# Weights that land in place in a two-loop attention layer, a bias that goes through DRAM, and two orders on TensorE

## The chip, the cores and the metric

One core of a Trainium2 chip runs the whole program. The metric is the device time of one execution in microseconds (us), lower is better. The kernel before takes 3244.75 us, the median of three runs (3242.59 to 3246.57).

## The reference, cut to what matters

One inference step of two layers, for a prompt of 2048 rows and a sample of 32 rows, in float32, model width 1024.

Layer 0 (here "layer AB"): an RMS norm, one input projection `h @ w_in`, then two head groups on the result.

- Group A is a gated linear attention: 4 heads, keys of 64, values of 128, a low-rank decay gate (`glow @ w_gate_up + b_gate`, log-sigmoid, divided by 16), a state that is carried from rows to rows, a per-head RMS norm and a SiLU gate z_a.
- Group B is a sliding-window attention: 8 query heads of 64, 2 key heads, window 128, scores plus a relative-position bias (a table of 32 buckets by 8 heads), a softmax with a learned sink, a SiLU gate z_b.
- The outputs of both are concatenated, multiplied by `w_out` and added to x.

```
h = rms_norm(x, rms_g)
q_a, k_a, v_a, glow, z_a, q_b, k_b, v_b, z_b = _split(h @ w_in, SPLIT_AB)
s = einsum(q, k) * HD_B ** -0.5 + bias ;  p = sink_softmax(s, sink)
return x + concat([o_a * silu(z_a), o_b * silu(z_b)]) @ w_out, ...
```

Layer 1 (a Mamba-2 block) follows. It takes the larger part of the time, and no instruction of it is changed.

## The kernel before, in words

The rows are worked on in 17 tiles: tile 0 is the sample (32 rows), tiles 1 to 16 are 128 rows of the prompt each. The program runs in blocks one after another, each with its own semaphores, with a barrier of all engines between two (`give_back`): `setup`, `layer_gla` (group A, here "the first loop"), `layer_swa` (group B and the output projection, "the second loop"), `layer_c`, `project_c`. Data goes from block to block through DRAM.

Each engine's order is written out by hand as `start(x, n)`, 16 times `step(x, n, m)` and `end(x)`; x is the tile that is finished, n the next, m the one after that. SP issues all transfers of the loops, in this order too, and a wait in SP's list holds up all that stands behind it. Engines wait on counters: `since(pe, s["za_made"], x, 1)` waits until the tile before x has been through that stage.

A float32 product of full accuracy is made from three products of rounded operands: high by high, high by low, low by high. So each weight matrix is split once: ScalarE (ACT) writes the high half (`weights_high`, a Copy that rounds, for `w_in` with the norm's scale), and VectorE (DVE) writes the low half, raw minus high (`weights_low`). The raw rows come in through a staging buffer, one k of 8 (128 of the 1024 rows) at a time:

- First loop: 1808 columns, `stage_a` with three places. ACT issues the first three k in `setup`; SP issues the other five in `layer_gla`, each once the low half of the k three before is made (L342). In `project`, TensorE (PE) waits in the sample's first product for the low half of each k.
- Second loop: 1024 columns of `w_in`, then `w_out`, through two places that are a view of `sc`, the tile of the attention scores (`stage`, L853). So the first scores of the loop wait for all 16 low halves. SP's list has the load of tile 1 (`load_h(n)`) behind all of them.

`setup` also makes the bias: PE and DVE build `frep`, a row of offsets per head; SP writes it to DRAM (`skew`), waits, and reads it back shifted by one element per partition into `bias`; DVE adds the band mask, and the block ends.

Orders on PE that the change touches:

- First loop, `step`: `queries_keys(n)`, `attention(x)`, `values(n)` (gate columns into bank VG, then the values into bank V0), `gate_low(n)`, `outputs(x)`, `turn_qk(n)`, `gate_up(n)`, `turn_x(m)`, `gate(n)` (z_a, in the same bank as the queries and keys), `turn_oa(x)`. `queries_keys(n)` waits for `za_made` of the tile before, DVE's last read of that bank.
- Second loop, `step`, where `before` is the tile before x: `scores(x)`, `queries(n)`, `turn_weights(x, 0)`, `turn_x1(before)`, `gate(n)`, `steps_in(before)` (L1472, reads h1T, which DVE writes), `turn_weights(x, 1)`, `weighted(x, 0)`, `time_step(before)`, `output_start(x, 0)`, `weighted(x, 1)`, `output_start(x, 1)`, `turn_ob(x)`, `turn_q(n)`, `turn_k(n)`, `output_end(x)`. ACT's list after `steps_in` is: `time_step(before)`, `window_gate(n)` with two table loads, then `weights_turned(x, 1)`, the copy that `weighted(x, 1)` reads. DVE's is: `weights_turned(x, 1)`, `weighted(x, 0)`, `time_step_tok(before)`, `window_gate(n)`, `weighted(x, 1)`.

## Time and profile before

| what | value |
|---|---|
| median of three runs | 3244.75 us |
| the profiled execution | 3245.2 us, its span 3243.4 us |
| TensorE: matmul busy, weight load busy | 2931.4 us (90%), 2485.5 us (77%) |
| DVE, ACT, POOL busy | 1876.6 (58%), 1412.8 (44%), 61.3 us (2%) |
| mean granted TensorE clock | 0.968 |
| DMA | 87 GB/s over the span |

The span runs from the first instruction to the last. A line of a timeline gives start and duration in us, the engine, the source line, the operation, what it writes and reads, and in brackets how long its engine was idle before it and what ended that. SPq is SP's own list. A matmul's duration is longer than its distance to the next one, because matmuls overlap; the pace is read from the starts. "issue" as a releaser means that the profile shows nothing the engine waited for. The blocks begin at these times: the first loop at 34.13 us, its 16 steps at about 88 us, the second loop at 557.84 us, layer 1 at 1355.76 us.

### The profile page before, as it was taken

Reading aid. Unit: us, or ns where it says so; the run is one execution under the profiler, and the core shown is the slowest. Engines: PE = TensorE matmul, PEld = TensorE weight load, DVE = VectorE, ACT = ScalarE, POOL = GpSimd, SP = SyncE. Lnnn points to the kernel's source line nnn. Section 1 sums busy time; section 2 is a strip of 40 time slices with the busy share of each in tenths; the row PEclk is TensorE's granted clock in tenths of the full one; section 3 lists DMA queues with packets and bytes.
Section 4 is the critical chain, followed back from the end, with each engine's and each line's share of the span. In section 5 each row is a group of like instructions: output and inputs, shape, how many; then the busy total and the mean of one; then the engine's idle time right before and its main releaser. Section 6 shows DMA issues by size and latency. Waiting matters only on the chain. (4 is left out here: it accounts for less than half of the span.)

```text
span 3243.4 us, 50025 instructions
## 1 busy us (share of the span) xinstructions
PE 2931.4 (90%) x18074; PEld 2485.5 (77%) x18074; DVE 1876.6 (58%) x4799; ACT 1412.8 (44%) x2901; POOL 61.3 (2%) x166
## 2 busy tenths in 40 slices
PE   4999996688888888599999999999999999879999
PEld 2788886266666666489997999889997999758787
DVE  3343343344443444268887888878887888842322
ACT  2455553333333333245555555545555555521211
POOL 0000000000000000000000000000000000000000
PEclk9999998699999999799999999999999999989999
DMA  4122212322212221332213221142123211144443
GB/s 144 71 83 82 82 71 71 122 73 82 82 65 75 79 80 59 127 114 65 64 60 102 83 64 59 51 133 65 59 62 100 66 61 60 53 170 137 131 145 111
DMA packets 148699, 280.87 MB, mean 87 GB/s; under 512 B 46359, under 2 KB 69402, under 8 KB 144378
## 3 DMA queue, kind: packets, MB, share of 16 engines
q1 hardware_dynamic: 147042, 276.55, 26.0%
q10 hardware_dynamic: 1560, 3.05, 0.3%
q8 instruction: 58, 0.95, 0.1%
q14 instruction: 39, 0.32, 0.0%
HBM read 204.29 MB, written 75.26 MB: 86 GB/s over the span
## 5 line engine op out<-in xcount | busy, mean ns | idle before, releaser
L2060 PEld LDWEIGHTS bank<-hT_c,w_group 128*128 128x128 f32 x6528 | 749.5, 192 | 39.1 <-issue 33.5
L2060 PE MATMUL bank<-hT_c,w_group 128*128 128x128 f32 x6528 | 750.9, 275 | 0.0
L1884 DVE SCALAR_TENSOR_TENSOR conv_acc<-u,convw,conv_acc 128x128 f32<-128x128 f32 (+1 forms) x1224 | 331.4, 339 | 10.4 <-ACT conv_acc L1818 8.0
L2047 PE MATMUL bank<-wz_high,h_high 128*128 128x512 f32 (+1 forms) x544 | 239.2, 440 | 13.5 <-DVE wz_low L1965 13.5
L708 PE MATMUL bank<-wa_high,hT_high 128*128 128x512 f32 (+5 forms) x544 | 191.0, 351 | 43.2 <-DVE za L622 26.0
L2285 PE MATMUL bank<-wout_high,yT_high 128*128 128x512 f32 (+1 forms) x544 | 212.6, 391 | 6.4 <-DVE wout_low L2254 6.4
L2047 PE MATMUL bank<-wz_low,h_high 128*128 128x512 f32 (+1 forms) x544 | 215.3, 396 | 0.0
L2047 PE MATMUL bank<-wz_high,h_low 128*128 128x512 f32 (+1 forms) x544 | 214.9, 395 | 0.0
L2285 PE MATMUL bank<-wout_low,yT_high 128*128 128x512 f32 (+1 forms) x544 | 212.5, 391 | 0.0
L2285 PE MATMUL bank<-wout_high,yT_low 128*128 128x512 f32 (+1 forms) x544 | 212.5, 391 | 0.0
L708 PE MATMUL bank<-wa_low,hT_high 128*128 128x512 f32 (+5 forms) x544 | 187.2, 344 | 0.0
L708 PE MATMUL bank<-wa_high,hT_low 128*128 128x512 f32 (+5 forms) x544 | 187.1, 344 | 0.0
L2218 ACT ACTIVATE yT_high<-yT_in 128x2048 fp32r<-128x2048 f32 (+1 forms) x34 | 62.6, 1841 | 275.1 <-PE bank L2285 260.8
L1772 ACT ACTIVATE u<-bank 128x256 f32<-128x256 f32 (+1 forms) x68 | 25.5, 376 | 323.0 <-PE bank L2060 323.0
L1818 ACT ACTIVATE conv_acc<-u,vec,convw 128x128 f32<-128x128 f32 (+1 forms) x408 | 162.4, 476 | 7.0 <-ACT u L1772 3.0
L2262 DVE TENSOR_TENSOR x_in<-x_in,bank 128x512 f32<-128x512 f32 (+1 forms) x34 | 23.4, 687 | 220.6 <-PE bank L2285 220.6
L708 PEld LDWEIGHTS bank<-wa_high,hT_high 128*128 128x128 f32 (+1 forms) x544 | 100.3, 184 | 64.5 <-issue 34.1
L1434 PE MATMUL bank<-wout_high_ab,oT_high 128*128 128x512 f32 (+1 forms) x272 | 110.6, 407 | 38.6 <-DVE oT_low L1221 20.6
L1385 PE MATMUL bank<-wb_high,h0T_high 128*128 128x512 f32 (+1 forms) x272 | 117.2, 431 | 29.7 <-DMA h0T_low<-h0T_low_d 20.4
L2047 PEld LDWEIGHTS bank<-wz_high,h_high 128*128 128x128 f32 (+1 forms) x544 | 101.7, 187 | 51.8 <-issue 30.6
L2103 PE MATMUL bank<-xdt,ed 128*128 128x128 f32 (+1 forms) x1088 | 132.7, 275 | 3.1 <-DVE ed L1941 3.1
L2103 PEld LDWEIGHTS bank<-xdt,ed 128*128 128x128 f32 (+1 forms) x1088 | 125.9, 187 | 5.6 <-DVE ed L1941 5.3
(289 smaller groups left out, 5812.1 us busy)
## 6 DMA issues: line engine op xcount, KB each, us to landing
hT_c<-h1T SPq DMA_DIRECT2D x64, 512.0 KB, 3.3
acb<-acT SPq DMA_DIRECT2D x64, 512.0 KB, 3.7
yT_in<-yT SPq DMA_DIRECT2D x32, 1024.0 KB, 5.2
yT<-yT_t SPq DMA_DIRECT2D x64, 256.0 KB, 3.1
xin<-in_x_prompt SPq DMA_DIRECT2D x16, 512.0 KB, 3.7
h0T_high_d<-hT_high SPq DMA_DIRECT2D x16, 512.0 KB, 2.6
h0T_low_d<-hT_low SPq DMA_DIRECT2D x16, 512.0 KB, 3.4
h0T_high<-h0T_high_d SPq DMA_DIRECT2D x16, 512.0 KB, 3.4
```

The costliest lines, as they stand in the source:

```text
L708: ins = M(out, h[x.buf][:, k, 0:x.R], wt[:, k, col:col + n], start=(k == 0 and p == 0), stop=(k == KT - 1 and p == 2))
L1385: ins = M(out, h[:, k, 0:x.R], wt[:, k, col:col + 512], start=(k == 0 and p == 0), stop=(k == KT - 1 and p == 2))
L1434: ins = M(B_OUT[n][0:x.R, :], y[:, k, 0:x.R], wt[:, k, 512 * n:512 * n + 512], start=(k == 0 and p == 0), stop=(k == KT - 1 and p == 2))
L1772: A(ub[:, 4:6, 3:3 + R], B_BC[:, 0:2 * P].rearrange("p (j r) -> p j r", j=2)[:, :, 0:R], ACT.Copy).then_inc(s["u1_made"], 1)
L1818: ins = A(acc[:, i, 0:R], ub[:, i, 3:3 + R], ACT.Identity, scale=c["convw"][:, 3 * CT + ct:3 * CT + ct + 1], bias=c["vec"][:, V_CB + ct:V_ ...
L1884: ins = V.scalar_tensor_tensor(acc[:, i, 0:R], ub[:, i, tap:tap + R], c["convw"][:, tap * CT + ct:tap * CT + ct + 1], acc[:, i, 0:R], ALU. ...
L2047: ins = M(B_Z[0:x.R, :], h[:, k, 0:x.R], wt[:, k, :], start=(k == 0 and p == 0), stop=(k == KT - 1 and p == 2))
L2060: ins = M(out, wg[x.g % 2][:, k, j * P:(j + 1) * P], hT[x.buf][:, k, :], start=(k == 0), stop=(k == KT - 1))
L2103: ins = M(B_INTRA[h // 4][0:R, (h % 4) * P:(h % 4 + 1) * P], ed[0:R, h, 0:R], xdt[0:R, (h // 2) * P:(h // 2 + 1) * P], start=True, stop=True)
L2218: nc.scalar.activation(yh[x.buf][:, :, 0:x.R], yT[x.buf][:, :, 0:x.R], ACT.Copy).then_inc(s["y_high"], 1)
L2262: V.tensor_tensor(x[0:R, :], x[0:R, :], psum[cur.buf][0:R, :], ALU.add).then_inc(s["sum_made"], 1)
L2285: ins = nc.tensor.matmul(psum[i][0:R, :], y[:, k, 0:R], wt[:, k, :], start=(k == 0 and p == 0), stop=(k == K - 1 and p == 2))
```

## The change

- The raw weights of the first loop get a tensor for all 8 k (`raw_a`), which lies at the address of the low half (`two_views`: one tensor is given back, and the other allotted in its place). DVE then writes the low half over the raw rows. SP and ACT issue all 8 k in `setup`, SP the even and ACT the odd ones. The sample's rows are loaded there too.
- The same for the second loop: `raw_b` is allotted for both loops. SP loads all 8 k of `w_in`'s other columns in `start` of the first loop, behind `store_h(n)` and ahead of step 0. Once the low half of a k is made, `w_out` of that k is loaded into the same place, where its low half will lie. `sc` is no staging buffer any more.
- `frep` is a view of `raw_b`. ACT writes it to DRAM at the end of `setup` and nothing there waits for it. `bias` and `band` are read in `start` of the second loop, and POOL adds them.
- First loop on PE: the gate columns are a stage of their own, `values_gate`, ahead of `queries_keys`; it needs no `za_made`.
- Second loop on PE: `steps_in(before)` goes behind `weighted(x, 0)`, `time_step(before)` behind `weighted(x, 1)`; the wait for `dtok_made` goes from `output_start(x, 0)` to `output_start(x, 1)`.

```diff
+def two_views(nc, stack, raw, low, shape):
+    with ExitStack() as first:
+        r = first.enter_context(nc.sbuf_tensor(raw, shape, F32))
+    return r, stack.enter_context(nc.sbuf_tensor(low, shape, F32R))
...
+            w["raw_b"], w["wout_low"] = two_views(nc, ab, "wb_raw", "wout_low_ab", [P, KT, DM])
...
+                w["raw_a"], w["wa_low"] = two_views(nc, gla, "wa_raw", "wa_low", [P, KT, A_W])
...
@@ setup @@
+        def weights(eng, k):
+            raw = w["raw_a"][:, k, :]
+            eng.dma_start(raw[:, 0:QB], wv[k][:, 0:QB]).then_inc(c["wa_in"][k], 16)
+            eng.dma_start(raw[:, QB:A_W], wv[k][:, KB:ZB]).then_inc(c["wa_in"][k], 16)
...
-            sp.wait_ge(s["offsets_copied"], HB)
-            sp.dma_start(d["skew"], frep[:, :, :]).then_inc(s["skew_out"], 16)
-            sp.wait_ge(s["skew_out"], 16)
...
-            sp.dma_start(w["bias"][:, :, :], skewed).then_inc(s["bias_in"], 16)
+            sp.dma_start(w["xin"][0:DEC, :], a["x_sample"][0]).then_inc(c["x_in"], 16)
+            for k in range(0, KT, 2):
+                weights(sp, k)
...
-            dve.wait_ge(s["bias_in"], 16)
-            nc.vector.tensor_tensor(w["bias"][:, :, :], w["bias"][:, :, :],
-                                    band[:, :].unsqueeze(1).to_broadcast([P, HB, 2 * P]), ALU.add).then_inc(s["set_dve"], 1)
...
+            for k in range(1, KT, 2):
+                weights(act, k)
             act.wait_ge(s["params_in"], 16 * n_in)
             nc.scalar.activation(c["acol"][:, :], alog[:, :], ACT.Exp).then_inc(s["exp_a"], 1)
+            act.wait_ge(s["offsets_copied"], HB)
+            act.dma_start(d["skew"], frep).then_inc(c["skew_out"], 16)
@@ layer_gla, SP @@
+            def next_weights():
+                sp.wait_ge(c["skew_out"], 16)
+                for k in range(KT):
+                    raw = w["raw_b"][:, k, :]
+                    sp.dma_start(raw[:, 0:512], wv[k][:, QB:KB]).then_inc(c["wb_in"][k], 16)
+                    sp.dma_start(raw[:, 512:DM], wv[k][:, ZB:D_AB]).then_inc(c["wb_in"][k], 16)
...
             def start(x, n):
-                load_x(x)
...
                 load_x(n)
-                for k in range(3, KT):
-                    weights(k)
                 store_h(x)
                 store_kv(x)
                 store_h(n)
+                next_weights()
@@ layer_gla, PE @@
             def start(x, n):
...
+                values_gate(x)
                 queries_keys(x)
                 values(x)
...
             def step(x, n, m):
+                values_gate(n)
                 queries_keys(n)
                 attention(x)
                 values(n)
@@ layer_swa, SP @@
             def weights(k):
-                if k >= 2:
-                    sp.wait_ge(s["w_low"], k - 1)
...
+                sp.wait_ge(s["w_low"], k + 1)
+                sp.dma_start(raw[:, k, :], wo[k]).then_inc(wo_in[k], 16)
...
             def start(x, n):
                 load_h(x)
-                weights(0)
-                weights(1)
                 load_kv(x)
...
-                for k in range(2, KT):
-                    weights(k)
+                sp.dma_start(bias[:, :, :], skewed).then_inc(s["bias_in"], 16)
+                sp.dma_start(band[:, :], a["c_band"]).then_inc(s["bias_in"], 16)
                 load_oa(x)
                 residual(x)
-                for k in range(KT, 2 * KT):
+                for k in range(KT):
                     weights(k)
@@ layer_swa, POOL @@
+            pool.wait_ge(s["bias_in"], 32)
+            nc.gpsimd.tensor_tensor(bias[:, :, :], bias[:, :, :],
+                                    band[:, :].unsqueeze(1).to_broadcast([P, HB, 2 * P]), ALU.add).then_inc(s["bias_made"], 1)
+            pool.wait_ge(s["bias_made"], 1)
+            nc.gpsimd.tensor_copy(bprev[:, :, :], bias[:, :, 0:P]).then_inc(s["init0"], 1)
@@ layer_swa, DVE scores @@
                 if x.sample:
-                    dve.wait_ge(s["w_low"], 2 * KT)
+                    dve.wait_ge(s["bias_made"], 1)
@@ layer_swa, PE @@
             def output_start(x, n):
                 if n == 0:
                     pe.wait_ge(s["oa_in"], 32 * x.t + 32)
+                    since(pe, s["h2_half"], x, 1, 2)
+                else:
                     since(pe, s["dtok_made"], x, 1)
-                    since(pe, s["h2_half"], x, 1, 2)
                 partial(x, n, 0)
...
                 gate(n)
-                if before is not None:
-                    steps_in(before)
                 turn_weights(x, 1)
                 weighted(x, 0)
                 if before is not None:
-                    time_step(before)
+                    steps_in(before)
                 output_start(x, 0)
                 weighted(x, 1)
+                if before is not None:
+                    time_step(before)
                 output_start(x, 1)
```

## Rows read from the trace of the kernel before

**Rows 1.** Windows, second loop's steps: length, busy per engine, clock, DMA share, GB/s
```profile
640.00:1340.00 700.00, 592.71 (x3028) 465.20 (x3026) 290.68 (x684) 233.24 (x606) 31.49 (x49) 0.97 0.21 73
```

**Rows 2.** Waits of PE, 0 to 600 us: sum, times, longest
```profile
PE bank L708 <- DVE za L622: 26.0, 16, 1.7
```

**Rows 3.** Waits of PE, 640 to 1340 us
```profile
PE bank L1472 <- DVE h1T_t L1250: 50.0, 16, 3.4
...
PE bank L1434 <- issue: 18.0, 16, 1.2
```

**Rows 4.** Timeline, end of setup and start of the first loop
```profile
21.09 0.13 DVE L229 TENSOR_SCALAR acol<-acol 32x1 f32<-32x1 f32 x1
...
31.06 2.29 DVE L232 TENSOR_TENSOR bias<-bias,band 128x2048 f32<-128x2048 f32 x1 [9.84 <-DMA bias<-skew]
...
36.49 1.06 ACT L421 ACTIVATE xn<-xin 32x1024 f32<-32x1024 f32 x1 [1.07 <-DMA xin<-in_x_sample]
```

**Rows 5.** Timeline, the first loop's weights
```profile
43.29 6.13 DVE L565 SCALAR_TENSOR_TENSOR wa_low<-stage_a,vec,wa_high 128x1808 fp32r<-128x1808 f32 x3 [1.40 <-ACT wa_high L414]
...
66.61 2.10 DVE L565 SCALAR_TENSOR_TENSOR wa_low<-stage_a,vec,wa_high 128x1808 fp32r<-128x1808 f32 x1 [1.99 <-ACT wa_high L414]
...
69.20 0.63 PE L708 MATMUL bank<-wa_low,hT_high 128*32 128x512 f32 x1
...
73.46 0.42 PE L708 MATMUL bank<-wa_high,hT_high 128*32 128x272 f32 x1
...
74.71 0.28 PE L744 MATMUL bank<-wa_high,hT_high 128*32 128x256 f32 x1
```

**Rows 6.** Timeline, a step of the first loop
```profile
311.34 1.28 DVE L579 TENSOR_TENSOR hT_low<-bank,hT_high 128x512 fp32r<-128x512 f32 x2
...
315.29 0.47 PE L708 MATMUL bank<-wa_high,hT_high 128*128 128x512 f32 x1 [1.64 <-DVE za L622]
```

**Rows 7.** Timeline, tile 2's rows in step 0
```profile
90.73 1.06 ACT L421 ACTIVATE xn<-xin 128x1024 f32<-128x1024 f32 x1 [0.40 <-DMA xin<-in_x_prompt]
```

**Rows 8.** Windows, five us of bulk loads at the start of layer 1
```profile
1365.00:1370.00 5.00, 1.08 (x3) 0.52 (x4) 1.92 (x4) 2.58 (x5) 0.00 (x0) 0.50 1.05 394
```

**Rows 9.** Timeline, start of the second loop
```profile
557.84 1.28 ACT L1102 ACT_TABLE_LOAD   x1 [5.67 <-PEq L65]
...
565.19 1.28 DVE L1163 SCALAR_TENSOR_TENSOR wb_low<-sc,vec,wb_high 128x1024 fp32r<-128x1024 f32 x1 [12.23 <-ACT wb_high L1013]
...
567.32 0.69 PE L1499 MATMUL bank<-ident,kdup 128*128 128x128 f32 x2 [15.87 <-DMA wdt<-in_w_in_c]
...
596.03 0.43 PE L1486 MATMUL bank<-ident,qn 32*128 32x32 f32 x4
...
599.79 2.36 DVE L1166 TENSOR_TENSOR wout_low_ab<-sc,wout_high_ab 128x1024 fp32r<-128x1024 f32 x2 [2.10 <-ACT wout_high_ab L1015]
...
620.90 1.67 DVE L1179 TENSOR_TENSOR sc<-bank,bias 32x320 f32<-32x320 f32 x4
...
623.04 0.79 PE L1385 MATMUL bank<-wb_high,h0T_high 128*128 128x512 f32 x1 [20.44 <-DMA h0T_low<-h0T_low_d]
...
630.39 0.55 PE L1415 MATMUL bank<-ident,sc 32*128 32x32 f32 x8
```

**Rows 10.** Timeline, a step of the second loop
```profile
932.36 1.94 PE L1472 MATMUL bank<-h1T_t,wdt 128*32 128x128 f32 x16 [3.02 <-DVE h1T_t L1250]
...
934.23 1.09 PE L1415 MATMUL bank<-ident,sc 128*128 128x128 f32 x8
...
938.47 0.47 PE L1434 MATMUL bank<-wout_high_ab,oT_high 128*128 128x512 f32 x1 [1.12 <-issue]
...
938.60 0.60 ACT L1039 ACTIVATE pT<-bank 128x512 f32<-128x512 f32 x1
...
941.32 0.38 PE L1425 MATMUL bank<-vprev,pT 128*128 128x128 f32 x2
...
943.02 0.48 PE L1434 MATMUL bank<-wout_high_ab,oT_high 128*128 128x512 f32 x1
```

More of the change, by code:

```diff
@@ L137, in program @@
         c["wc_in"] = nc.alloc_semaphore("wc_in")
-        c["wa_in"] = [nc.alloc_semaphore(f"wa_in{i}") for i in range(3)]
+        c["wa_in"] = [nc.alloc_semaphore(f"wa_in{i}") for i in range(KT)]
+        c["wb_in"] = [nc.alloc_semaphore(f"wb_in{i}") for i in range(KT)]
+        c["x_in"], c["skew_out"] = nc.alloc_semaphore("x_in"), nc.alloc_semaphore("skew_out")
         with ExitStack() as ab:
             w = {}
-            w["bias"] = sb("bias", [P, HB, 2 * P], ab)
-            w["wdt"] = sb("wdt", [P, KT, HC], ab)
+            w["raw_b"], w["wout_low"] = two_views(nc, ab, "wb_raw", "wout_low_ab", [P, KT, DM])
             with ExitStack() as gla:
                 w["wup"] = sb("wup", [RANK, HA * DK], gla)
-                w["stage_a"] = sb("stage_a", [P, 3, A_W], gla)
+                w["xin"] = sb("xin", [P, DM], gla)
+                w["raw_a"], w["wa_low"] = two_views(nc, gla, "wa_raw", "wa_low", [P, KT, A_W])
                 give_back(nc, setup(nc, a, c, d, w, psum))
@@ L340, in _ @@
             wv = a["w_in_ab"][0].rearrange("(k p) n -> k p n", p=P)
-            def weights(k):
-                sp.wait_ge(s["w_low"], k - 2)
-                sp.dma_start(stage[:, k % 3, 0:QB], wv[k][:, 0:QB]).then_inc(w_in[k % 3], 16)
-                sp.dma_start(stage[:, k % 3, QB:A_W], wv[k][:, KB:ZB]).then_inc(w_in[k % 3], 16)
+            def next_weights():
[4 more added lines that the diff above has]
+                    sp.dma_start(raw[:, 512:DM], wv[k][:, ZB:D_AB]).then_inc(c["wb_in"][k], 16)
             def load_x(x):
-                if not x.fixed or x.t > 0:
-                    sp.wait_ge(s["xn_made"], x.t)
-                sp.dma_start(xin[0:x.R, :], a["x_sample"][0] if x.sample else xp[x.t - 1]).then_inc(s["x_in"], 16)
+                sp.wait_ge(s["xn_made"], x.t)
+                sp.dma_start(xin[0:x.R, :], xp[x.t - 1]).then_inc(c["x_in"], 16)
             def store_h(x):
@@ L738, in attention, with values_gate @@
                 ins.then_inc(s["kd_full"], 1)
+            def values_gate(x):
+                pe.wait_ge(s["h_low"], 2 * x.t + 2)
+                project(B_VG[0:x.R, 0:A_VG], x, A_V1, A_VG, s["vg_full"])
             def values(x):
-                project(B_VG[0:x.R, 0:A_VG], x, A_V1, A_VG, s["vg_full"])
                 for k in range(KT):
@@ L832, in sb @@
             return ctx.enter_context(nc.sbuf_tensor(name, shape, dtype))
-        bias, wdt = w["bias"], w["wdt"]
-        bprev = sb("bprev", [P, HB, P])
+        bias, bprev, band = sb("bias", [P, HB, 2 * P]), sb("bprev", [P, HB, P]), sb("band", [P, 2 * P])
+        wdt = sb("wdt", [P, KT, HC])
         wh, wl = sb("wb_high", [P, KT, DM], F32R), sb("wb_low", [P, KT, DM], F32R)
-        vh, vl = sb("wout_high_ab", [P, KT, DM], F32R), sb("wout_low_ab", [P, KT, DM], F32R)
+        vh, vl = sb("wout_high_ab", [P, KT, DM], F32R), w["wout_low"]
+        raw = w["raw_b"]
         hh, hl = sb("h0T_high", [P, KT, P], F32R), sb("h0T_low", [P, KT, P], F32R)
@@ L1010, in weights_high @@
             def weights_high(k):
-                act.wait_ge(w_in[k % 2], 32 * (k // 2 + 1))
                 if k < KT:
-                    A(wh[:, k, :], stage[:, k % 2, :], ACT.Copy, scale=c["vec"][:, V_RMS0 + k:V_RMS0 + k + 1]).then_inc(s["w_high"], 1)
-                else:
-                    A(vh[:, k - KT, :], stage[:, k % 2, :], ACT.Copy).then_inc(s["w_high"], 1)
+                    act.wait_ge(c["wb_in"][k], 32)
+                    A(wh[:, k, :], raw[:, k, :], ACT.Copy, scale=c["vec"][:, V_RMS0 + k:V_RMS0 + k + 1]).then_inc(s["w_high"], 1)
+                else:
+                    act.wait_ge(wo_in[k - KT], 16)
+                    A(vh[:, k - KT, :], raw[:, k - KT, :], ACT.Copy).then_inc(s["w_high"], 1)
             def softmax(x, half):
```

53 lines of the change are left out of this document (18 added, 35 removed).

## The prediction

> **What bounds the kernel now.** I read the windows by stage first, then PE's waits, then the timeline of single steps. Layer AB ends at 1352 us of 3243, and nothing after it is changed, so only what moves its end counts. In the second loop's steps [rows 1] PE's matmuls are busy 592.7 of 700 us, DVE 290.7, ACT 233.2, DMA a fifth: PE sets the pace there and the others count only where PE waits for them. PE's waits in the steps are few and regular: 26.0 us in 16 waits for `za` in the first loop [rows 2]; 50.0 us in 16 for h1T and 18.0 us in 16 for "issue" in the second [rows 3]. The last are at `output_start(x, 0)`, where PE really waits for `dtok_made`: the matmul starts at 938.47 [rows 10], 0.11 us after DVE's copy ends. The two starts are different: there PE idles for tens of us behind weights that come in through few staging places. So three things can be won: setup and the first start, the second start, and the steps' waits.
>
> **Setup and start of the first loop.** The last work of the block now is the bias, which ends at 31.06 + 2.29 = 33.35; without it DVE's small instructions end at 21.22 [rows 4]: 12.1 us earlier. The readback, 9.84 us of that, goes to the second loop. x of the sample is loaded in setup, so ACT's wait of 1.07 goes [rows 4]. What is late next is ACT's norm of that tile, unchanged. Then the weights: from DVE's first low half at 43.29 to its last at 66.61 + 2.10 = 68.71 pass 25.4 us. DVE's pace without waits is 6.13 / 3 = 2.04 [rows 5], so eight take 16.3, if all eight are there: 7.4 MB from 5.5 us on at about 390 GB/s [rows 8] are in after 19 us, at 24.5, and DVE's first low half is due at 43.29 - 12.1 - 1.1 = 30.1. That makes 9.1 more, and the last low half at 46.4. On the other side stands the order on PE. Before, the 24 matmuls of 512 columns ran between the low halves and only one group of three was left; now the 24 of 272 columns do, and the 24 of 512 come behind the last low half. PE paces them at 0.43 us (half clock, 69.20 against its neighbours) until it has worked without a gap from 68.7 to 73.5; after that 0.23 [rows 5]. So: 0.7 for the last group, to 47.1; 9.5 matmuls at 0.43 until 51.2; 14.5 at 0.23, to 54.6. The values start there, against 74.71 [rows 5]: 20.1 us won. Bounds: 22.3 if PE is quick at once, 15 if ACT, which now issues half the weights and the skew, is held up by a full queue.
>
> **Steps of the first loop.** `values_gate(n)` needs `h_low` alone, which DVE has made at 311.34 + 1.28 = 312.6, while PE comes free at 315.29 - 1.64 = 313.65 [rows 6]. It runs 24 x 0.125 = 3.0 us, and `za` is made at 315.1, inside that. So all 26.0 us [rows 2] go. What is late next: `gate_low(n)` waits for ACT's copy of the gate columns, which comes behind ACT's norm of tile m (its x lands late in each step) and two copies; by the timeline ACT is through about 2.5 us before PE asks. Bounds 16 (if that margin is wrong by one us in each step) and 28. I take 26.0.
>
> **The preload of 4 MB.** Its 16 issues on SP stand ahead of `load_x` of tile 2. They need 4.2 MB / 390 GB/s = 10.7 us [rows 8], then that tile 1.4, and x lands some 8.2 us later relative to its step than at 90.7 [rows 7]. ACT is in order: norm (3.7 us), then copies of queries, keys, gate. PE does not ask for the gate's copy before it is through 24 + 24 + 48 matmuls, so of 8.2 us I find 0.5 left on the path. Every further us of landing time costs one. Loss 0.5, bounds 0 and 7 (at 275 GB/s, as just after the start of the second loop, it is 15 us). The preload is over by step 1.
>
> **Start of the second loop.** Weights are there. ACT begins after its table load, at 557.84 + 1.28 = 559.1; low halves at DVE's pace of 1.28 [rows 9] are ready from 561.6 to 570.7. PE needs the small loads before: the last of these (`wdt`) is the eleventh issue of the block and released PE at 567.32 [rows 9]; with four weight issues (2.2 us) less ahead, 565.1. Queries and gate of the sample are 48 matmuls: 11 at 0.43, 37 at 0.23, 13.2 us, so PE's `turn_q` at 578.7 against 596.03 [rows 9]: 17.3 won. ACT then starts the high halves of `w_out` at 581.4 (2.7 later, as before), and all of `w_out` has landed: its loads are issued from 565 to 571 and need 11 us. DVE started its first at 599.79 and its second ended 2.36 later, 1.18 each [rows 9]: first at 582.5, eight end at 591.9, and scores start there instead of 620.90: 29.0 won. SP is free to send `load_h(1)` right after `vcur` is copied (581.0 instead of 617.2), so `queries(1)`, 7.3 us long (623.04 to 630.3), ends at 594.7. Then PE waits for the exponentials: scores to exponentials took 5.5 us on DVE and ACT, so `turn_weights(0)` is at 597.4 instead of 630.39 [rows 9]: 33.0 won. The bias lands near 569, and POOL's add, which DVE did in 2.29 [rows 4], is wanted at 591.9: hidden by 15 us or more. Bounds 26 (loads of small rows as slow as before, `w_out` at 275 GB/s) and 36.
>
> The Trainium skill speaks against this add: "SBUF — State Buffer", section "Who interferes with whom", says that a DVE instruction with two SBUF inputs and a GpSimd one that reads SBUF lock each other out for a whole instruction, and "GPSIMD Engine Reference", section "Performance versus the Vector engine", gives 4.5 us for the add. By these the seventh or eighth low half would end some 4 us later and PE's queries 2.2 us, and the forecast would be 3149; no row of before shows two such instructions at once.
>
> **Steps of the second loop.** Now PE waits 3.02 us for h1T, until 932.36 [rows 10]. `turn_weights(x, 1)` (0.92) and `weighted(x, 0)` (1.8) move in there; ACT and DVE have made what they need at 929.6. So `steps_in` starts at 932.4 as before and ends at 934.23. `output_start(x, 0)`, 12 matmuls or 2.85 us (938.47 to 941.32), ends at 937.1. But `weighted(x, 1)` needs ACT's copy that starts at 938.60 and takes 0.60 [rows 10], and this hangs on `steps_in` through ACT's time step and two table loads, which do not move. PE waits 2.1 us there, starts at 939.25, and with 1.70 (941.32 to 943.02) is through at 940.95. `time_step(before)` and DVE's copy of `dtok` make 0.8 more, and `output_start(x, 1)` starts at 941.8 against 943.02 [rows 10]: 1.24 us per step, 15 steps with a tile before: 18.6. In `end` the order stays and only the wait for `dtok` (1.1) is covered: 1.1. Sum 19.7. Bounds: 0, and 4.1 x 15 = 62, if neither wait came back.
>
> **Sum.** 20.1 + 26.0 - 0.5 + 33.0 + 19.7 = 98.3. From the profiled execution's 3245.2, 0.45 above the median, that is 3146.9: 3147.
>
> **Rivals.** *The transfers bound it* (12%): they gain at most where queues have room. For it: SP's issues of large loads at the start of layer 1 stood for up to 6 us each. ACT's skew then leaves only when the weights are in (24.5 instead of 20.4, 4 us), the preload runs at 275 GB/s (5 us), and `w_out` and the small loads give back 7: 3163. Against it: loads of 128 long rows were issued at 0.45 to 0.85 us. *Nothing comes out of the second loop's order* (14%): PE's waits only move to `weighted(x, 1)` and `dtok`, as DVE and ACT, in order, shift with PE: 3147 + 18.6 = 3166. *Both waits go* (8%), if ACT's copy is earlier than I read: 43 us better, 3104. *It does not do what it says* (2%): if the raw tensors are not free when their loads are issued, setup waits anyway; then the starts' 53 us are gone, 3200. *Slower* (2%): the new wait of 2.1 us ahead of `weighted(x, 1)`, inside a stretch that had short waits only, drops PE's clock to half. A step has 13.6 us of matmuls from there to the next scores' end; at half clock 15 steps cost 204 us and the time is 3351. It decides from 6.5 us of work at half clock per step on (98.3 / 15). Against it: the wait of 3.02 us at about the same place leaves the clock at 0.97 [rows 1].
>
> **How the numbers follow.** The forecast, 3147 with its own range of 3128 to 3162, has 62%. A measurement here tells 0.2% (6.5 us) from no change. All cases but the last are faster by more than that: faster 97%; slower 2%; 1% for a mixture that ends within. The range of 8 in 10 takes in the second rival and the first: 3125 to 3178.
>
> **What would show it.** Right: `norm` of the sample at 23.4 us; last low half of the first loop near 46.4; no wait for `za`; second loop's block about 45 us earlier and its first scores at DVE 34 us after the block's start (63 before); PE's wait for h1T under 0.4 us, and a new one of about 2 us for ACT's `pT`. Wrong: ACT's x wait in step 0 over 12 us; a step of the second loop of 41.8 us as before; a clock under 0.9 in a loop.

## The result, and the profile after

The changed kernel takes 3149.84 us (median of 4, 3145.83 to 3151.18) against 3243.67 for the kernel before (median of 4, 3238.45 to 3246.57): a ratio of 0.971, 95% interval 0.9694 to 0.9727. The forecast was 3147. Its profiled execution took 3149.56 us with a span of 3147.8, against 3245.2 of before: 95.6 us less.

The sum comes out within 3 us, but two of its terms are wrong in opposite directions. All times in this table are read from the two profiled executions, as the distance between the same event before and after. `oa_high` is ACT's copy of a tile's finished outputs of group A, one per tile, so the distance of two is one step of the first loop:

```
                               predicted   measured
setup and first start            20.1        19.5
first loop's steps               26.0        30.2   (16 x 1.89)
preload of 4 MB in step 0        -0.5       -10.3
second start                     33.0        33.2
second loop's steps              19.7        27.2
layer 1 (unchanged)               0          -4.2
sum                              98.3        95.6
```

The preload's term is what closes the balance at the first `oa_high`, 11.2 us earlier than before (107.44 against 118.65). The start gave 19.5 and step 0 its share of the steps' term, about 2.0, so 19.5 + 2.0 - 11.2 = 10.3 were lost on the way. Experiment 1 measures it directly. From its first matmul to the end, layer 1 took 1884.4 us before and 1888.6 after; over the profiled executions of all twelve kernels, which have the same code there, it is 1881.7 to 1888.7. So the last term is scatter of that size.

**First start.** The timeline after, end of setup and the first loop's weights (start, length, engine, line, operation; in brackets the wait ahead of it), answers [rows 4, 5]:

```profile
23.50 1.05 ACT L423 ACTIVATE xn<-xin 32x1024 f32<-32x1024 f32 x1
...
30.30 16.19 DVE L567 SCALAR_TENSOR_TENSOR wa_low<-wa_raw,vec,wa_high 128x1808 fp32r<-128x1808 f32 x8 [1.40 <-ACT wa_high L416]
...
47.23 0.63 PE L710 MATMUL bank<-wa_high,hT_high 128*32 128x512 f32 x1
...
52.35 0.50 PE L710 MATMUL bank<-wa_high,hT_high 128*32 128x512 f32 x1
...
55.22 0.28 PE L748 MATMUL bank<-wa_high,hT_high 128*32 128x256 f32 x1
```

The norm starts at 23.50 (23.4 was forecast), all eight low halves are one row without a gap, 16.19 long, and end at 46.49 (46.4). The 24 matmuls of 512 columns start at 47.23, the pace turns from 0.43 to 0.23 at 52.35, and the values start at 55.22 instead of 74.71.

**First loop's step.** From one tile's `oa_high` to the next it is 26.19 us now (317.12 to 343.31, for one). This window is as long as one step: length, busy time of PE, PE's weight loads, DVE, ACT, POOL, clock, DMA share, GB/s.

```profile
311.34:337.53 26.19, 26.19 (x173) 23.57 (x172) 10.91 (x34) 14.57 (x38) 0.00 (x0) 1.00 0.23 85
```

PE is busy in all of it. The wait for `za`, 26.0 us in 16 before [rows 2], is gone, and the step takes 26.19 instead of 28.08.

**Step 0, where the preload lies.** SP's queue and then ACT and PE:

```profile
66.41 0.79 SPq L350 DMA_DIRECT2D wb_raw<-in_w_in_ab  x1
67.24 1.19 SPq L351 DMA_DIRECT2D wb_raw<-in_w_in_ab  x1
...
75.11 0.45 SPq L351 DMA_DIRECT2D wb_raw<-in_w_in_ab  x1
75.60 0.44 SPq L355 DMA_DIRECT2D xin<-in_x_prompt  x1
```

The waits of PE in the first loop after (engine, line, what it waited for: sum, times, longest), and windows behind the first of them:

```profile
PE bank L755 <- ACT v_tok L448: 4.6, 1, 4.6
```
```profile
88.40:93.00 4.60, 4.55 (x17) 1.52 (x17) 0.00 (x0) 0.73 (x2) 0.00 (x0) 0.50 0.08 29
93.00:98.00 5.00, 5.00 (x17) 3.35 (x16) 1.54 (x5) 1.87 (x10) 0.00 (x0) 0.50 0.00 0
98.00:103.00 5.00, 5.00 (x21) 4.28 (x20) 4.31 (x14) 4.83 (x15) 0.00 (x0) 0.76 0.00 0
103.00:108.00 5.00, 5.00 (x32) 4.23 (x31) 3.21 (x9) 2.96 (x4) 0.00 (x0) 1.00 0.54 211
```

The 16 issues hold SP from 66.41 to 75.56, so x of tile 2 is issued at 75.60; ACT, in order, stands for it 12.9 us, until 83.7. ACT's copy of the gate columns (L448) comes behind it, and PE waits 4.6 us for that copy. Then it runs at half clock (0.50, the lower of its two levels) for 9.6 us, and for part of the next five, in which the mean is 0.76. The granted clock, the last figure but two of a row, is the one to read: PE is "busy" in all of it.

**Second start.** Timeline after, answering [rows 9]:

```profile
518.44 1.28 ACT L1106 ACT_TABLE_LOAD   x1 [5.41 <-PEq L65]
...
525.13 0.69 PE L1504 MATMUL bank<-ident,kdup 128*128 128x128 f32 x2 [12.83 <-DMA wdt<-in_w_in_c]
...
529.59 5.46 POOL L981 TENSOR_TENSOR bias<-bias,band 128x2048 f32<-128x2048 f32 x1 [10.05 <-DMA band<-in_c_band]
...
539.04 0.44 PE L1491 MATMUL bank<-ident,qn 32*128 32x32 f32 x4
...
542.80 9.58 DVE L1170 TENSOR_TENSOR wout_low_ab<-wb_raw,wout_high_ab 128x1024 fp32r<-128x1024 f32 x8 [2.10 <-ACT wout_high_ab L1019]
...
546.63 0.50 PE L1389 MATMUL bank<-wb_high,h0T_high 128*128 128x512 f32 x1 [2.55 <-DMA h0T_low<-h0T_low_d]
```

From the block's start at 518.44 it is 6.7 us to PE's release by `wdt` (7.3 forecast), 20.6 to `turn_q` (20.9), 24.4 to the first low half of `w_out` (24.7), and `turn_weights(0)`, at 557.79, is 39.4 us after the start (39.6 forecast; 72.6 before). Only `queries(1)` came by another way: PE waited 2.55 us for its rows and ran at half clock for 3.3, but the exponentials were later still.

**Second loop's step.** Timeline of one step after, answering [rows 10], and PE's waits from 560 to 1270 us, answering [rows 3]:

```profile
852.60 1.93 PE L1477 MATMUL bank<-h1T_t,wdt 128*32 128x128 f32 x16 [0.47 <-DVE h1T_t L1254]
...
858.83 0.60 ACT L1043 ACTIVATE pT<-bank 128x512 f32<-128x512 f32 x1
...
859.48 0.49 PE L1429 MATMUL bank<-vprev,pT 128*128 128x128 f32 x2 [2.01 <-ACT pT L1043]
...
862.09 0.50 PE L1438 MATMUL bank<-wout_high_ab,oT_high 128*128 128x512 f32 x1 [0.32 <-DVE dtok_t L1273]
```
```profile
PE bank L1429 <- ACT pT L1043: 29.8, 15, 2.0
...
PE bank L1477 <- DVE h1T_t L1254: 11.2, 16, 3.0
...
PE bank L1438 <- DVE dtok_t L1273: 4.7, 15, 0.3
```

The wait for h1T shrank from 3.02 to 0.47 (under 0.4 forecast), and the new one for ACT's `pT` is 2.01 (2.1 forecast). The steps take 40.8 to 41.05 us, but for one of 43.76. Before, they were of two kinds: 41.8 to 42.2 and, in about two of three, 43.3 to 43.8. One of the long kind in windows, then the five us in which h1T is waited for and the five behind them, all of the kernel before:

```profile
946.47:990.21 43.74, 37.38 (x190) 29.52 (x189) 18.27 (x43) 14.78 (x39) 1.95 (x3) 0.96 0.22 76
970.00:975.00 5.00, 1.70 (x11) 1.12 (x10) 4.25 (x13) 0.95 (x3) 0.00 (x0) 0.99 0.54 177
975.00:980.00 5.00, 5.00 (x31) 4.26 (x30) 1.23 (x4) 2.12 (x4) 0.00 (x0) 0.67 0.34 138
```

Behind the wait the clock is 0.67 in the mean, that is, at half for some 3.3 of the five us. The steps without a drop went from about 42.0 to 40.9 us, so the change took 1.1 us of waits out of each, and nearly everywhere this drop too, 1.7 us in each long step. The forecast had only the first.

The one long step of the changed kernel shows that the new wait can bring a drop as well. It is this wait for `pT` with the matmuls behind it, and the whole step:

```profile
652.08 0.49 PE L1429 MATMUL bank<-vprev,pT 128*128 128x128 f32 x2 [1.99 <-ACT pT L1043]
```
```profile
655.00:660.00 5.00, 4.68 (x12) 3.62 (x12) 1.15 (x3) 0.00 (x0) 0.21 (x1) 0.50 0.03 7
627.83:671.59 43.76, 39.07 (x191) 30.79 (x189) 18.17 (x44) 14.78 (x38) 1.96 (x3) 0.92 0.22 72
```

### The profile page after: what moved, and what is told of

It is laid out like the page before. It is cut to its first block and busy times, and to the rows that moved or that the text cites. A ratio compares the mean times of both kernels' runs of the same rounds, so it can differ in the third digit from the quotient of the medians.

```text
span 3147.8 us, 50003 instructions
## 1 busy us (share of the span) xinstructions
PE 2924.8 (93%) x18074; PEld 2485.2 (79%) x18074; DVE 1870.8 (59%) x4798; ACT 1411.4 (45%) x2901; POOL 67.9 (2%) x167
## 5 line engine op out<-in xcount | busy, mean ns | idle before, releaser
L2052 PE MATMUL bank<-wz_high,h_high 128*128 128x512 f32 (+1 forms) x544 | 240.0, 441 | 12.9 <-DVE wz_low L1970 12.9
L2267 DVE TENSOR_TENSOR x_in<-x_in,bank 128x512 f32<-128x512 f32 (+1 forms) x34 | 23.4, 687 | 219.8 <-PE bank L2290 219.8
L1438 PE MATMUL bank<-wout_high_ab,oT_high 128*128 128x512 f32 (+1 forms) x272 | 112.7, 414 | 25.3 <-DVE oT_low L1225 20.6
L2052 PEld LDWEIGHTS bank<-wz_low,h_high 128*128 128x128 f32 (+1 forms) x544 | 102.0, 188 | 35.4 <-issue 14.4
L2290 PEld LDWEIGHTS bank<-wout_high,yT_high 128*128 128x128 f32 (+1 forms) x544 | 99.7, 183 | 32.0 <-DVE yT_low L2253 5.4
```

The costliest lines, as they stand in the source:

```text
L1438: ins = M(B_OUT[n][0:x.R, :], y[:, k, 0:x.R], wt[:, k, 512 * n:512 * n + 512], start=(k == 0 and p == 0), stop=(k == KT - 1 and p == 2))
L2052: ins = M(B_Z[0:x.R, :], h[:, k, 0:x.R], wt[:, k, :], start=(k == 0 and p == 0), stop=(k == KT - 1 and p == 2))
L2267: V.tensor_tensor(x[0:R, :], x[0:R, :], psum[cur.buf][0:R, :], ALU.add).then_inc(s["sum_made"], 1)
L2290: ins = nc.tensor.matmul(psum[i][0:R, :], y[:, k, 0:R], wt[:, k, :], start=(k == 0 and p == 0), stop=(k == K - 1 and p == 2))
```

## Experiments

Ratios are to the kernel before, timed beside it. The kernels are edits of the changed one, unless said otherwise. "A" and "B" are the accounts of each experiment's own expectation.

**1. The preload behind x of tile 2.** The 16 issues move from the end of `start` to behind `load_x(m)` of step 0.

```diff
@@ SP, start
-                next_weights()
@@ SP, step
                     load_x(m)
+                if x.fixed and x.t == 0:
+                    next_weights()
```

> The changed kernel with the preload of the second loop's 4 MB issued behind the load of tile 2's rows instead of ahead of it; nothing else differs. Theory A (the preload delays x of tile 2 by 8 us, PE stands 4.6 us in step 0, and its clock then falls to half for about 10 us, some 4 to 5 us more): ACT's wait of 12.9 us for x falls to about 0.5, PE's wait in step 0 goes, and the time falls by 8 to 10 us, to about 3141. Rival B (only the wait costs; the slow stretch behind it comes anyway): it falls by 4.6 us. Rival C (4 MB of transfers beside the first loop slow it wherever they are): nothing changes, or the wait appears in step 1.

Measured: 3138.77 us (3136.3 to 3141.93), ratio 0.9673 [0.9656, 0.9689]: 11.1 less than the changed kernel. The first `oa_high` is at 97.12 instead of 107.44, 10.3 earlier. Timeline and windows of this kernel:

```profile
66.08 0.79 SPq L355 DMA_DIRECT2D xin<-in_x_prompt  x1
71.73 1.06 ACT L424 ACTIVATE xn<-xin 128x1024 f32<-128x1024 f32 x1 [1.25 <-DMA xin<-in_x_prompt]
```
```profile
70.00:75.00 5.00, 5.00 (x29) 4.34 (x28) 0.63 (x4) 2.81 (x6) 0.00 (x0) 1.00 1.03 386
75.00:80.00 5.00, 5.00 (x40) 4.27 (x39) 0.29 (x1) 1.64 (x4) 0.00 (x0) 1.00 1.05 386
80.00:85.00 5.00, 5.00 (x40) 3.99 (x39) 0.00 (x0) 0.74 (x2) 0.00 (x0) 1.00 0.31 115
```

x lands 12 us earlier, the same 4 MB are moved at 386 GB/s beside a PE that is always busy at clock 1.00. So the preload costs TensorE nothing in itself; its place in SP's queue cost about 10 us.

**2. The first loop's order undone** in the steps only; `start` keeps the new one.

```diff
@@ PE, queries_keys
+                pe.wait_ge(s["h_low"], 2 * x.t + 2)
@@ PE, step
-                values_gate(n)
                 queries_keys(n)
                 attention(x)
+                values_gate(n)
```

> The changed kernel with the order of the first loop's steps as before: queries and keys, attention, then the gate columns. The order in start and all else stay changed. Theory A (the order is worth PE's wait for za, 1.64 us, and 0.25 us of work at the pace it has right behind the wait, per step): the steps take 28.1 us again instead of 26.19, PE waits 26 us for za, and the time rises by 27 to 29 us, to about 3178. Rival B (the shorter step comes from transfers and memory that are quieter now that weights are not loaded in the loop): the steps stay under 27 us and the time rises by less than 10 us.

Measured: 3178.06 (3173.89 to 3179.13), ratio 0.9793 [0.9776, 0.981]: 28.2 us more than the changed kernel. Steps are 28.08 again, and PE waits as before:

```profile
PE bank L710 <- DVE za L624: 24.1, 15, 1.6
```

1.89 a step: 1.6 is the wait. That the other 0.25 is PE's slower pace on resuming is by difference only.

**3. Both edits of the second loop's order undone** (`steps_in` ahead of `turn_weights`, `time_step` ahead of `output_start(x, 0)`, the wait for `dtok_made` back there).

```diff
@@ PE, output_start
                 if n == 0:
                     pe.wait_ge(s["oa_in"], 32 * x.t + 32)
+                    since(pe, s["dtok_made"], x, 1)
                     since(pe, s["h2_half"], x, 1, 2)
-                else:
-                    since(pe, s["dtok_made"], x, 1)
@@ PE, step
+                if before is not None:
+                    steps_in(before)
                 turn_weights(x, 1)
                 weighted(x, 0)
                 if before is not None:
-                    steps_in(before)
+                    time_step(before)
                 output_start(x, 0)
                 weighted(x, 1)
-                if before is not None:
-                    time_step(before)
```

> The changed kernel with both edits of the second loop's order undone (steps_in ahead of turn_weights 1, time_step ahead of output_start 0, with the wait for dtok there). Theory A (the order is worth 1.1 to 1.2 us of waits per step, and besides it keeps PE's clock up, which falls to half for part of two steps in three before, 1.7 us each): steps of 41.9 and 43.7 us come back, granted clock 0.96 in the long ones, and the time rises by 26 to 30 us, to about 3178. Rival B (the clock dips before came from something else, such as the state in which the loop is entered): all steps take about 42.0 us, clock 1.00, and the time rises by 17 us, to 3167.

Measured: 3179.58 (3170.42 to 3182.8), ratio 0.9794 [0.9771, 0.9817]: 29.7 more than the changed kernel, where the table's term is 27.2 and the forecast's 19.7. The two kinds of steps are back, 41.9 to 42.1 at clock 1.00 and 43.4 to 43.9 at 0.96 (one of 44.7 at 0.92). The rival in which nothing comes out of this order (3166 in the forecast) is out.

**4. Only `steps_in` moved back.**

```diff
@@ PE, step
+                if before is not None:
+                    steps_in(before)
                 turn_weights(x, 1)
                 weighted(x, 0)
-                if before is not None:
-                    steps_in(before)
                 output_start(x, 0)
```

> The changed kernel with only steps_in moved back ahead of turn_weights 1; time_step and the wait for dtok stay where the change put them. Theory A (weighted 1 is bound by ACT's copy of pT, which hangs on steps_in whatever stands between; the place of steps_in by itself moves no end): PE waits 3.0 us for h1T again, the wait for pT falls from 2.0 to 0, and a step takes 40.9 to 41.0 us if the clock stays up, 3150. If the wait of 3.0 us is what drops the clock, the steps alternate with ones 1.7 us longer at a clock of 0.96, and the time is 3160 to 3168. Rival B (each filled wait is a gain by itself): steps of 43 us, 3180.

Measured: 3184.05 (3173.41 to 3189.49), ratio 0.982 [0.9801, 0.984]. That is the time of both edits undone, within what runs scatter, and more than account A expected (3160 to 3168); by the time alone the rival, 3180, would have it. The waits moved as A says: 51.8 us in 17 for h1T, none for `pT`. But every step now shows a drop of the clock, and a few are longer again: 42.5 to 43.0 us at 0.96, and three of 44.1 to 44.2 at 0.92. Two steps one behind the other:

```profile
669.41:712.40 42.99, 37.42 (x190) 29.70 (x189) 18.28 (x44) 14.81 (x38) 1.96 (x3) 0.96 0.23 80
712.40:756.48 44.08, 38.57 (x190) 30.58 (x189) 18.27 (x44) 14.81 (x38) 1.96 (x3) 0.92 0.23 76
```

Length times clock gives 41.3 and 40.6. So by this estimate a step at full clock would take about 41 us, as in the changed kernel: it is the clock that makes it longer, and not the place of `steps_in` by itself. Experiment 6 tests that. This `steps_in` is PE's row right behind the wait:

```profile
903.67 3.27 PE L1477 MATMUL bank<-h1T_t,wdt 128*32 128x128 f32 x16 [3.23 <-DVE h1T_t L1254]
```

It takes 3.27 us where it takes 1.93 in the changed kernel.

**5. Only `time_step` moved back**, and the wait for `dtok_made` with it.

```diff
@@ PE, output_start
                     pe.wait_ge(s["oa_in"], 32 * x.t + 32)
+                    since(pe, s["dtok_made"], x, 1)
                     since(pe, s["h2_half"], x, 1, 2)
-                else:
-                    since(pe, s["dtok_made"], x, 1)
@@ PE, step
                     steps_in(before)
+                    time_step(before)
                 output_start(x, 0)
                 weighted(x, 1)
-                if before is not None:
-                    time_step(before)
```

> The changed kernel with steps_in where the change put it, but time_step right behind it and the wait for dtok at output_start 0, as before. Theory A (the gain in waits comes from output_start 0 no longer standing behind dtok; steps_in's place alone shortens no chain): PE waits about 2.4 us for the time step and 1.1 for dtok instead of 2.0 for pT, output_start 0 begins about 0.2 us earlier than in the kernel before, and a step takes 41.7 us if the clock stays up: 3150 + 15 x 0.9 = 3163. If these waits drop the clock in steps, up to 1.7 us more in each. Rival B (steps_in's place is what brings the gain): steps of 41.0 us, 3150.

Measured: 3179.56 (3177.57 to 3182.78), ratio 0.9808 [0.9792, 0.9824]. Steps 42.5 to 43.0 and 44.0 to 44.1; PE's waits:

```profile
PE bank L1484 <- DVE dtac L1268: 38.3, 16, 2.5
```

Account A of this expectation had a step of 41.7 us at full clock. Measured are 42.98 at a clock of 0.96 and 44.03 at 0.92, for two steps one behind the other, which makes 41.3 and 40.5: as far as this estimate goes, the rival's 41.0, and A's 41.7 is wrong.

So each of the two edits by itself is worth nothing in the time. The step at full clock is about 41 us with either, but one wait of 3.2 us in front of `steps_in` (experiment 4) or of 2.4 in front of `time_step` (here, 38.3 in 16) stays, and the clock falls in every step. Together they split it into 0.5 and 2.0 us, and only one step shows a drop.

**6. The wait filled with useless work.** Kernel 4 again, with 11 matmuls of 128x512 into a bank that is not in use, put where PE would wait for h1T; nothing reads them.

```diff
@@ PE, step, on top of kernel 4
                 gate(n)
                 if before is not None:
+                    pe.wait_ge(s["sc_added"], 4 * x.t + 4)
+                    for k in range(11):
+                        M(B_PT[2][:, :], vh[:, k % KT, 0:P], wh[:, k % KT, 0:512], start=True, stop=True)
                     steps_in(before)
```

> The kernel with steps_in moved back ahead of turn_weights 1, and 11 matmuls of 512 columns without use ahead of it, in PE's wait of 3.0 us for h1T; they write a bank that is free there. Theory A (the wait of 3 us is what drops the clock in each step, 1.7 us of PE's time every time): no step with a clock under 1.00, steps of 40.9 to 41.1 us, and the time falls from 3184 to about 3150, though PE does 11 matmuls more per step. Rival B (the clock falls for another cause, or steps_in's place costs 1.7 us by itself): the time stays at 3175 to 3190 or rises.

Measured: 3152.53 (3151.1 to 3154.86), ratio 0.9721 [0.9705, 0.9737]: 31.5 us less than kernel 4, with more work on the engine that bounds it. (Kernel 4 was profiled in the fastest of its executions, 3173.41; between the two profiles layer 1 starts 20.1 us earlier.) Steps are 41.1 to 41.4 but for one of 43.53, and the row to compare with that of kernel 4 is

```profile
895.42 1.93 PE L1477 MATMUL bank<-h1T_t,wdt 128*32 128x128 f32 x16 [0.75 <-DVE h1T_t L1254]
```

The data that `steps_in` waits for, ACT, DVE and the transfers are as in kernel 4; only most of PE's idling is gone, and with it the drop. So the drop hangs on PE's idling. But not every such wait brings it. In the one long step of this kernel h1T came late, and PE waited as long as before the change, at full clock:

```profile
1145.31 0.30 PE L1477 MATMUL bank<-h1T_t,wdt 128*32 128x128 f32 x1 [3.02 <-DVE h1T_t L1254]
```
```profile
1145.00:1150.00 5.00, 4.70 (x41) 4.50 (x42) 1.55 (x5) 2.63 (x5) 0.00 (x0) 1.00 0.26 105
```

The steps of 41.8 to 42.2 us of the kernel before also had their wait of 3 us and no drop, and the changed kernel has a drop behind one of its waits of 2.0. What decides it in the single step, these runs leave open.

**7. `pT` copied earlier.** The wait of 2.0 us that the change left hangs on ACT's order, so ACT's and DVE's parts of `weights_turned(x, 1)` move ahead of the time step.

```diff
@@ ACT, step
                 weights_turned(x, 0)
+                weights_turned(x, 1)
                 if before is not None:
                     time_step(before)
                 window_gate(n)
-                weights_turned(x, 1)
@@ DVE, step
                     turned_x1(before)
-                    time_step(before)
                 weights_turned(x, 1)
+                if before is not None:
+                    time_step(before)
```

> The changed kernel with the copies that weighted 1 waits for put earlier in the lists of ACT (right behind the copy of half 0, ahead of the time step and of the window gate with its two table loads) and of DVE (right behind h1T, ahead of the time step). Theory A (after the change PE's wait of 2.0 us in each step is for ACT's place of this copy and nothing else): the wait for pT goes, h1T's and dtok's small waits stay, a step takes 38.9 to 39.2 us against 40.9, and the time falls by 25 to 30 us, to about 3122. Rival B (DVE's chain of h1T or the time step takes the place of the wait, since both lists are in order): the step falls by less than 0.8 us.

Measured: 3108.73 (3106.96 to 3110.68), ratio 0.9589 [0.9573, 0.9605]: 41 us less than the changed kernel, where 25 to 30 were expected. Steps are 38.4 to 38.9, the wait for `pT` is gone and no step shows a drop; the waits for h1T (11.2 in 16) and `dtok` (4.7 in 15) stay. In the profiled executions layer 1 starts 35.7 us earlier; the rest lies in layer 1, whose code is the same (1881.7 us against 1888.6). This is the forecast's rival "both waits go" (3104), reached by the edit that it would have needed.

**8. The two orders alone**, put on the kernel before, with the definitions and waits that belong to them and with the gate columns first in the first loop's `start` too; storage and loads stay as before.

```diff
@@ PE, first loop's step, on the kernel before
+                values_gate(n)
                 queries_keys(n)
                 attention(x)
@@ PE, second loop's step, on the kernel before
-                if before is not None:
-                    steps_in(before)
                 turn_weights(x, 1)
                 weighted(x, 0)
                 if before is not None:
-                    time_step(before)
+                    steps_in(before)
                 output_start(x, 0)
                 weighted(x, 1)
+                if before is not None:
+                    time_step(before)
```

> The kernel before with only the two orders on PE of the change (the gate columns first, in start too, and the second loop's three edits); weights, bias and all transfers as before. Theory A (orders and placement of the weights add up): the first loop's steps take 26.2 us and the second's 40.9, worth 28 + 29 = 57 us, less 2 us in start: 3244 - 55 = 3189. Rival B (the orders pay only with the weights in place, or the placement has its gain from the shorter steps): the sum of the two parts differs from 94 us by more than 8.

Measured: 3186.36 (3182.06 to 3190.48), ratio 0.9831 [0.9814, 0.9847]. Against the kernel before, timed beside it (3241.63), the orders are worth 55.3 us without the new places of the weights. With them they are worth 28.2 + 29.7 = 57.9, by experiments 2 and 3. The two agree within what runs scatter, so the gain of the orders does not depend on the placing of the weights. For that some 37 us are left (3186.4 to 3149.8), where the table has 19.5 - 10.3 + 33.2 = 42.4, less the 4.2 of layer 1. One thing differs: in this kernel's profile none of the second loop's steps shows a drop of the clock, though each has the wait of 2.0 us for `pT`.

**9. Bias and band loaded first in the second start**, ahead of the sample's rows, so that POOL's add comes while DVE makes low halves. The kernel ran once.

```diff
@@ SP, start of the second loop
+                flat = d["skew"].rearrange("q h m -> (q h m)")
+                skewed = bass.AP(flat.tensor, flat.offset + P - 1, [[HB * REL - 1, P], [REL, HB], [1, 2 * P]])
+                sp.dma_start(bias[:, :, :], skewed).then_inc(s["bias_in"], 16)
+                sp.dma_start(band[:, :], a["c_band"]).then_inc(s["bias_in"], 16)
                 load_h(x)
                 load_kv(x)
...
-                sp.dma_start(bias[:, :, :], skewed).then_inc(s["bias_in"], 16)
-                sp.dma_start(band[:, :], a["c_band"]).then_inc(s["bias_in"], 16)
                 load_oa(x)
```

> The changed kernel with the loads of bias and band as the first ones of the second loop instead of behind wdt, so that POOL's add of 2048 elements falls into the time in which DVE writes the low halves from two SBUF tensors. Theory A (the Trainium skill's rule in 'SBUF - State Buffer', 'Who interferes with whom': such a pair lock each other out for a whole instruction): one or more low halves take or wait 2 to 5.5 us longer, the eighth ends near 535 in place of 530.6, or POOL's add is stretched well over the 5.46 us that it took. Theory B (no lock between them): DVE's eight low halves keep their 1.21 us each and POOL's add its 5.46. In both, PE's first small loads land some 3 us later; the time itself, 3150 to 3157, cannot tell them apart, the trace can.

Measured: 3155.31 us, one execution. The low halves and the add in this kernel (count, ns shortest/median/longest, first and last start):

```profile
L1167 DVE SCALAR_TENSOR_TENSOR wb_low<-wb_raw,vec,wb_high x8: 1272/1281/5552, 523.1 to 536.5; 128x1024 fp32r<-128x1024 f32 x8
...
L981 POOL TENSOR_TENSOR bias<-bias,band x1: 5292/5292/5292, 527.1 to 527.1; 128x2048 f32<-128x2048 f32 x1
```

One low half of eight takes 5.55 us: it starts at 527.90, 0.8 after the add, and ends 1.1 after it, about its own length of 1.28. Six take 1.28 and one 2.05, which starts at 533.37 beside POOL's next instruction, a copy of 1.92 us. In the changed kernel the add starts at 529.59, 0.3 after the last low half has begun, and the same row says 1279/1280/1284. So the low half does wait for the add. A DVE instruction with two SBUF inputs and a GpSimd one that reads SBUF exclude each other for a whole instruction: so says the Trainium skill, "SBUF — State Buffer", section "Who interferes with whom". This kernel agrees, with 5.55 us beside 5.29, for the DVE instruction that comes second, and the changed kernel escapes that by 0.3 us. That the add is held up by a low half is not shown: in the changed kernel it took 5.46, only 0.17 more, with 1.0 us of the low half still to go. Nor is a price in the time. From the block's start to `turn_weights(0)` it is 43.3 us here and 39.4 in the changed kernel, but PE's release by `wdt` is 3.9 us later too, as two more loads stand ahead of it, and that alone makes the difference. The one time of this kernel is 5.5 above the changed one's median.

**10. Three edits together:** those of 1 and 7, and queries ahead of the gate columns in the first `start` alone, so that the matmuls of 512 columns run between the low halves again.

```diff
@@ PE, start of the first loop, on top of 1 and 7
                 turn_x(x)
-                values_gate(x)
+                pe.wait_ge(s["h_low"], 2 * x.t + 2)
                 queries_keys(x)
+                values_gate(x)
```

> The changed kernel with three edits together: the copies for weighted 1 first in ACT's and DVE's lists, the preload behind tile 2's rows, and in start of the first loop queries and keys ahead of the gate columns. Theory A (all three act on different waits and add up): 3108.7 - 11 - 2 = 3096; the values of start begin 2.1 us earlier (at 53.1), no wait of 4.7 us in step 0, steps of the second loop of 38.6 us. Rival B (the preload's gain is lost, since the start is sooner over and the transfers then fall on something else): over 3102.

Measured: 3095.4 (median of 5, 3090.9 to 3102.37), before 3244.5, ratio 0.9544 [0.9529, 0.9559]. This is faster than both kernels, 54 us below the changed one. Experiments 1 and 7 gave 11.1 and 41.1, together 52.2, so the third edit gave nothing that can be told from scatter. Its own sign is there: `gate_low` of the sample comes 2.98 us earlier than in experiment 1 (57.54 against 60.52). But the first `oa_high` is at 97.27 against 97.12. Windows of this kernel:

```profile
78.00:83.00 5.00, 5.00 (x38) 3.40 (x37) 0.00 (x0) 0.74 (x2) 0.00 (x0) 1.00 0.21 76
83.00:88.00 5.00, 5.00 (x23) 3.85 (x23) 2.25 (x7) 2.89 (x13) 0.00 (x0) 0.65 0.00 0
88.00:93.00 5.00, 5.00 (x17) 4.01 (x16) 4.67 (x14) 4.52 (x13) 0.00 (x0) 0.67 0.00 0
```

The mean clock over these last 10 us is 0.66, so PE ran at half for about 7 of them, although it waits for nothing; the same work ran at 1.00 in experiment 1. The drop comes in a row of small matmuls that begins with the outputs of the sample's 32 rows. Why it falls in the one and not in the other is open.

## Why the prediction was right, and where not

- **Setup and first start: right.** 20.1 against 19.5, and each date on the way within 1.2 us. The step that could have gone wrong, giving up the overlap of the 512-column matmuls with the low halves, cost what was worked out.
- **First loop's steps: right mechanism, a little small.** The wait goes, nothing takes its place, and experiment 2 brings it back. Each step gives 1.89 and not 1.62.
- **The preload: the step that failed.** The forecast had x land 8.2 us later, "of 8.2 us I find 0.5 left on the path" and "every further us of landing time costs one". x was late by the issues (9.2 us) and by the transfers that were still ahead of it (8 from its issue to ACT's start, where it takes under 5.7 in experiment 1). That is some 12 us, and by the forecast's own slope about 4 us on the path: the 4.6 of PE's wait. What it did not have is the clock behind such a wait, which made 10 of 4.6. Experiment 1 gets all of it back. Two of the signs that the forecast gave for being wrong came here: ACT's wait for x was over 12 us (12.9), and the clock in a loop was under 0.9 (0.50 for 9.6 us). For the same reason the second loop's block began 39.4 us earlier, and not about 45.
- **Second start: right.** 33.0 against 33.2, with the add hidden and the order of events as forecast; it was also right to keep the lock out of the sum, though by a margin of 0.3 us that nothing in the trace of before could promise, which is luck.
- **Second loop's steps: the mechanism right, the size not.** Predicted waits of 2.1 for `pT` and under 0.4 for h1T were measured as 2.0 and 0.5, and 1.24 us of waits won in each step as 1.1. The term was 19.7 and is 27.2 (29.7 by experiment 3), because the drop of the clock was left out. It stood in the rival "slower", in the sentence "the wait of 3.02 us at about the same place leaves the clock at 0.97". That was a mean over 700 us. In it were about nine steps with a drop behind the wait, as in the five us at 0.67. Taken step by step, this would have been worth 1.7 us in each.
- **The rivals.** "Transfers bound it" was partly true in step 0 alone. "Nothing from the second order" and "does not do it" are excluded by experiments 3 and 8. "Slower" did not come as a whole, but its mechanism did once: in one step of the changed kernel the wait of 2.0 us for `pT` is followed by half clock, and the step is 2.9 us longer. The waits of 3.2 and 2.4 us in experiments 4 and 5 are followed by it in every step. The price is 1.7 to 3.2 us a time and not the 13.6 that the rival had.

The two errors, 9.8 us too little for the preload and 11.7 too little gain in the steps of both loops, nearly cancel, and the 4.2 of layer 1 go the other way. That the forecast of 3147 came so close is luck; its single terms say more for it than its sum.

## What to carry to other kernels

Read the granted clock in windows of a few us behind every wait that repeats, not as a mean of the loop. Here a wait of 2.4 to 3.2 us cost 1.7 or more in clock wherever the clock fell behind it, and splitting it, or filling it with useless matmuls, took some 20 to 30 us out of fifteen steps. Put bulk loads for later behind the small load that the next step needs, in the queue that issues both. And when a wait on TensorE has been moved by a new order, look at what its releaser does ahead of it: two copies moved on ACT and DVE gave more (36 to 41 us) than the reordering on TensorE before them (27 to 30).

## What the runs showed of the hardware

- A kernel got 31.5 us faster (3184.05 to 3152.53; 20.1 between the two profiles) by 11 added matmuls a step that nobody reads.
- A wait of about the same length is followed by half clock in some steps and not in others: one of 3.02 us at clock 1.00 throughout (experiment 6), one of 1.99 with half clock behind it (the changed kernel, at 652 us).
- Two edits that were worth nothing one at a time were worth 30 us together: with `steps_in` back in its old place the time is 3184, with `time_step` back 3180, with both back 3180, with neither 3150.
- A DVE operation of 1.28 us took 5.55 when it started 0.8 us after POOL's add of 5.29.
- The clock fell to half for about 7 of 10 us (0.65 and 0.67 in two windows of five) in a stretch in which PE was busy without a gap (experiment 10).
- 4 MB of preload at 386 GB/s beside a busy PE cost nothing on TensorE (experiment 1, clock 1.00, PE 5.00 of 5.00 us).
